# Attention softmax with the sink as a padded score column, a negated row maximum, and one transpose for each differential head

## The reference, cut to what matters

```python
# sliding window, per head: the sink takes part in the softmax, and its column is dropped
scores = q @ k.T * HEAD_DIM ** -0.5 - slope * dist          # -inf where masked
p = jax.nn.softmax(jnp.concatenate([scores, sink], axis=-1), axis=-1)[..., :-1]
out = p @ v

# differential, per head: two maps of scores, one product with v
s = q[m] @ k[m].T * HEAD_DIM ** -0.5 - slope * dist          # m = 0, 1; -inf where masked
p = jax.nn.softmax(s, axis=-1)
p_diff = p[:, :, 0] - lam * p[:, :, 1]
out = rms_norm(p_diff @ v, subln_g) * (1.0 - lambda_init)
```

## The time and the profile before

| what | value |
|---|---|
| median of 3 runs | 833.9 us |
| span of the profiled execution, first to last instruction | 831.0 us |
| so around the span, against the median of the runs | 2.9 us |
| PE busy | 780.1 us, 94% |
| DVE / ACT / POOL busy | 611.5 / 451.4 / 286.6 us |
| DMA, mean over the span | 162 GB/s |
| stretch of the attention steps | about 423 to 517 us from the span's start |
| mean granted TensorE clock | 0.985 |

### The profile page before, as it was taken

One profiled execution on the slowest core, in us unless ns is written; L12 is line 12 of the kernel. 1 busy time (PEld: TensorE's weight loads), 2 busy tenths in 40 slices (PEclk: granted clock), 3 DMA queues, 4 the chain that ended last, 5 costly groups with the idle time before them and its releaser, 6 DMA issues.

```text
span 831.0 us, 17788 instructions
## 1 busy us (share of the span) xinstructions
PE 780.1 (94%) x6332; PEld 764.7 (92%) x6332; DVE 611.5 (74%) x1077; ACT 451.4 (54%) x768; POOL 286.6 (34%) x174
## 2 busy tenths in 40 slices
PE   5989899799999999999899998699999999999994
PEld 5889899799999999999888877699999999999994
DVE  5899986867888887335867686589999999953332
ACT  7444454556555654436644555576666666644440
POOL 0366554463211221444665320742221222221231
PEclk9999999999999999999899999999999999999998
DMA  8444453455545566444342322525555555555531
GB/s 280 138 159 171 179 188 123 165 176 185 177 179 192 181 217 217 171 160 147 104 150 102 102 77 77 177 98 182 184 185 187 177 178 187 188 206 179 180 124 50
DMA packets 37631, 134.98 MB, mean 162 GB/s; under 512 B 4432, under 2 KB 4688, under 8 KB 37584
## 3 DMA queue, kind: packets, MB, share of 16 engines
q1 hardware_dynamic: 37584, 134.34, 46.8%
HBM read 133.28 MB, written 1.05 MB: 162 GB/s over the span
## 4 chain that ended last, share of the span: by engine, by line
PE 47%; DVE 8%; POOL 2%; ACT 2%; issue 2%; DVEq 0%; POOLq 0%; ACTq 0%
PE bank L1560 15%; PE bank L1561 15%; PE bank L1562 15%; POOL sumsq L507 1%; DVE tmp L1325 1%; DVE neg_max L1369 1%; ACT prob L883 1%; DVE row_max L1365 1%; POOL X L613 1%; DVE neg_max L1372 1%; DVE score L1360 1%; PE bank L1765 1%; PE bank L1773 1%; PE bank L1764 1%; DVE w_lo L967 1%
## 5 line engine op out<-in xcount | busy, mean ns | idle before, releaser
L1560 PE MATMUL bank<-h_hi,w_hi 128*128 128x256 f32 x1424 | 410.2, 288 | 23.2 <-DVE h_lo L979 13.5
L1561 PE MATMUL bank<-h_lo,w_hi 128*128 128x256 f32 x1424 | 406.1, 285 | 0.0
L1562 PE MATMUL bank<-h_hi,w_lo 128*128 128x256 f32 x1424 | 405.8, 285 | 0.0
L494 POOL TENSOR_TENSOR w_lo<-raw,w_hi 128x1024 fp32r<-128x1024 f32 (+2 forms) x86 | 211.6, 2463 | 434.0 <-ACT w_hi L643 433.9
L1560 PEld LDWEIGHTS bank<-h_hi,w_hi 128*128 128x128 f32 x1424 | 276.4, 194 | 30.2 <-DVE w_lo L967 12.0
L643 ACT ACTIVATE w_hi<-raw 128x1024 fp32r<-128x1024 f32 (+2 forms) x246 | 261.7, 1066 | 74.5 <-PE bank L1562 71.4
L967 DVE TENSOR_TENSOR w_lo<-raw,w_hi 128x1024 fp32r<-128x1024 f32 (+1 forms) x160 | 207.4, 1298 | 109.8 <-ACT w_hi L643 109.7
L1561 PEld LDWEIGHTS bank<-h_lo,w_hi 128*128 128x128 f32 x1424 | 276.7, 194 | 0.0
L1562 PEld LDWEIGHTS bank<-h_hi,w_lo 128*128 128x128 f32 x1424 | 276.5, 194 | 0.0
L1560 PE MATMUL bank<-f_hi,w_hi 128*128 128x256 f32 x432 | 121.5, 281 | 0.9 <-DVE f_lo L1234 0.9
L1561 PE MATMUL bank<-f_lo,w_hi 128*128 128x256 f32 x432 | 121.4, 281 | 0.0
(11 more groups left out here) (188 smaller groups left out, 771.7 us busy)
## 6 DMA issues: line engine op xcount, KB each, us to landing
raw<-in_w_up SPq DMA_DIRECT2D x108, 512.0 KB, 3.2
raw<-in_w_in SPq DMA_DIRECT2D x54, 512.0 KB, 3.3
raw<-in_w_down SPq DMA_DIRECT2D x32, 512.0 KB, 3.3
raw<-in_w_down SPq DMA_DIRECT2D x16, 704.0 KB, 4.1
raw<-in_w_o SPq DMA_DIRECT2D x8, 512.0 KB, 3.3
raw<-in_w_gate SPq DMA_DIRECT2D x8, 512.0 KB, 3.4
raw<-in_w_out SPq DMA_DIRECT2D x8, 512.0 KB, 3.3
raw<-in_w_b_out SPq DMA_DIRECT2D x4, 512.0 KB, 3.2
```

The costliest lines, as they stand in the source:

```text
L494: nc.gpsimd.tensor_tensor(w_lo[s][:, 0:n], raw[s][:, 0:n], w_hi[s][:, 0:n].bitcast(f32), ALU.subtract).then_inc(lo_ready[s], 1)
L1560: nc.tensor.matmul(ps, wh, hi[:, k, :], start=start and n == 0, stop=False)
L1561: nc.tensor.matmul(ps, wh, lo[:, k, :], start=False, stop=False)
L1562: last = nc.tensor.matmul(ps, wl, hi[:, k, :], start=False, stop=stop and n == len(ks) - 1)
```

## The change

- The score tile becomes `score[P, 8, 390]`: 8 slots, each of three pieces of 130 columns. In a sliding-window slot the columns behind the first and the second piece hold the sink (or -1e30), written once by POOL in `fill_pads`, during the stage `gate`. The row maximum and the exponentials with their sums run over the pieces and the pads, so the sink is in both. `sink_exp` and its addition go.
- The maximum is made with `negate=True` and written to `neg_max`. The third operation (L1369, L1372) goes.
- The exponentials are written in place. The wait of the bias for a free tile is now one on the transposes of the map 8 before.
- For a differential head DVE combines the two maps before the transpose: `first + mixing * second`, with `mixing = -lambda * sum(first) / sum(second)`. So one set of three transposes, one copy by ACT, one product with the values and one scaling stand for two. The group's transposes wait for the combination (`mixed`).
- The numbers of the semaphores follow: there are 12 groups g in place of 16 maps for the transposes, copies, products and outputs. They keep the steps of the last map of their group.
- `y_sq` shares the two tiles `cg`, so ACT waits for its own squares before the stage `up2`.

```diff
+GROUP_END = list(range(N_SWA)) + list(range(N_SWA + 1, N_MAPS, 2))
+PIECE = P + 2
     for m in range(N_MAPS):
-        steps[m + 3]["score"], steps[m + 4]["trans"], steps[m + 5]["pv"] = m, m, m
+        steps[m + 3]["score"], steps[m + 4]["sums"] = m, m
+    for g, m in enumerate(GROUP_END):
+        steps[m + 4]["trans"], steps[m + 5]["pv"] = g, g
...
+        def block_cols(m):
+            if m < N_SWA:
+                return ((0, P + 1), (PIECE, 3 * PIECE - 2))
+            return ((0, P), (P, 3 * P))
+        def pieces(m):
+            step = PIECE if m < N_SWA else P
+            return score[:, m % N_SWA, 0:3 * step].rearrange("p (n k) -> p n k", n=3)[:, :, 0:P]
...
+            def fill_pads():
+                pool.wait_ge(unit_done, UNIT0["gate"])
+                pool.wait_ge(const_in, 32)
+                nc.gpsimd.memset(score[:, :, 2 * PIECE - 2:2 * PIECE], -MASKED).then_inc(pads_done, 1)
+                pool.wait_ge(pads_done, 1)
+                for col in (P, 2 * PIECE - 2):
+                    nc.gpsimd.tensor_copy(
+                        score[:, 0:N_SWA, col].rearrange("p (j g) -> p j g", g=2),
+                        sinks[:].rearrange("p (g j) -> p j g", g=2)).then_inc(pads_done, 1)
...
             def exps(m):
-                act.wait_ge(negmax_done, m + 1)
-                if m >= 2:
-                    act.wait_ge(trans_done, m - 1)
+                act.wait_ge(negmax_done, 2 * (m + 1))
...
-                if kind == "swa":
-                    nc.scalar.activation(sink_exp[:, m, :], neg_max[:, m, :], ACT.Exp,
-                                         bias=sinks[:, h:h + 1]).then_inc(sink_done, 1)
...
+            act.wait_ge(y_ss_done, 10)
             up2 = ("conv_w_2", "conv_b_2")
...
                 dve.wait_ge(bias_done, m + 1)
-                for b, (lo, hi) in enumerate(((0, P), (P, 3 * P))):
-                    nc.vector.reduce_max(row_max[:, m, b:b + 1], score[m % 2][:, lo:hi], axis=AX.X
-                                         ).then_inc(max_done, 1)
-                dve.wait_ge(max_done, 2 * (m + 1))
-                if kind == "swa":
-                    nc.vector.tensor_scalar(neg_max[:, m, :], row_max[:, m, :], sinks[:, h:h + 1],
-                                            -1.0, ALU.max, ALU.mult).then_inc(negmax_done, 1)
...
+                for b, (lo, hi) in enumerate(block_cols(m)):
+                    nc.vector.tensor_reduce(neg_max[:, m, b:b + 1], score[:, m % N_SWA, lo:hi],
+                                            axis=AX.X, op=ALU.max, negate=True).then_inc(negmax_done, 1)
...
+                nc.vector.reciprocal(rden[:, m, :], row_sum[:, m, :]).then_inc(den_done, 1)
+                if part == 0:
+                    return
+                dve.wait_ge(den_done, DEN[m - 1] + 1)
+                dve.wait_ge(lam_step, 3)
+                nc.vector.scalar_tensor_tensor(mixing[:, h, :], rden[:, m, :], neg_lam[:, 0:1],
+                                               row_sum[:, m - 1, :], ALU.mult, ALU.mult
+                                               ).then_inc(den_done, 1)
+                dve.wait_ge(den_done, DEN[m])
+                first, second = score[:, (m - 1) % N_SWA, :], score[:, m % N_SWA, :]
+                for b, (lo, hi) in enumerate(block_cols(m)):
+                    nc.vector.scalar_tensor_tensor(first[:, lo:hi], second[:, lo:hi],
+                                                   mixing[:, h, b:b + 1], first[:, lo:hi],
+                                                   ALU.mult, ALU.add).then_inc(mixed, 1)
...
-            def transposes(m):
-                pe.wait_ge(exp_done, 2 * (m + 1))
+            def transposes(g):
+                m = GROUP_END[g]
+                if m < N_SWA:
+                    pe.wait_ge(exp_done, 2 * (m + 1))
+                    source = pieces(m)
+                else:
+                    source = pieces(m - 1)
+                    pe.wait_ge(mixed, 2 * (g - N_SWA + 1))
```

More of the change, by code:

```diff
@@ L296, in build @@
         ev = [sb(f"ev{i}", [P, TOK]) for i in range(4)]
-        cg = [sb(f"cg{i}", [P, TOK]) for i in range(2)]
+        cg_pair = sb("cg", [P, 2 * TOK])
+        cg, y_sq = [cg_pair[:, i * TOK:(i + 1) * TOK] for i in range(2)], cg_pair
         cv = [sb(f"cv{i}", [P, TOK]) for i in range(2)]
@@ L329, in build @@
         v_a, v_b = place("v_a", [P, 2, P]), place("v_b", [P, 2, 512])
-        score = [place(f"score{i}", [P, 3 * P]) for i in range(2)]
-        prob = [place(f"prob{i}", [P, 3 * P]) for i in range(2)]
+        score = place("score", [P, N_SWA, 3 * PIECE])
         prob_T = [place(f"prob_T{i}", [P, 3 * P]) for i in range(2)]
@@ L334, in build @@
         y_hi, y_lo = place("y_hi", [P, DC, TOK], f32r), place("y_lo", [P, DC, TOK], f32r)
-        y_sq = place("y_sq", [P, 512])
-        row_max = place("row_max", [P, 16, 2])
         neg_max = place("neg_max", [P, 16, 2])
         row_sum = place("row_sum", [P, 16, 2])
-        sink_exp = place("sink_exp", [P, 16, 2])
-        denom = place("denom", [P, 16, 2])
         rden = place("rden", [P, 16, 2])
+        mixing = place("mixing", [P, 4, 2])
         y_ss = place("y_ss", [P, 5, 2])
@@ L557, in _ @@
                     power("gate")
+                    fill_pads()
                 if c > 0:
@@ L1375, in denominators @@
             def denominators(m):
-                kind, _, part = MAPS[m]
-                n = DEN[m - 1] if m else 0
+                kind, h, part = MAPS[m]
                 dve.wait_ge(exp_done, 2 * (m + 1))
[L1379 to L1385, removed]
@@ L1386, in denominators @@
-                nc.vector.reciprocal(rden[:, m, :], total).then_inc(den_done, 1)
-                if kind == "diff" and part == 1:
-                    dve.wait_ge(den_done, n + 1)
-                    dve.wait_ge(lam_step, 3)
-                    nc.vector.tensor_scalar(rden[:, m, :], rden[:, m, :], neg_lam[:, 0:1], None,
-                                            ALU.mult).then_inc(den_done, 1)
-            def scaled_output(m):
-                kind, h, part = MAPS[m]
-                dve.wait_ge(pv_done, m + 1)
+                nc.vector.reciprocal(rden[:, m, :], row_sum[:, m, :]).then_inc(den_done, 1)
@@ new lines, in denominators, with scaled_output @@
+                for b, (lo, hi) in enumerate(block_cols(m)):
+                    nc.vector.scalar_tensor_tensor(first[:, lo:hi], second[:, lo:hi],
+                                                   mixing[:, h, b:b + 1], first[:, lo:hi],
+                                                   ALU.mult, ALU.add).then_inc(mixed, 1)
+            def scaled_output(g):
+                kind, h, part = MAPS[GROUP_END[g]]
+                m, width = GROUP_END[g] - part, HD if kind == "swa" else P
+                dve.wait_ge(pv_done, g + 1)
@@ L1396, in scaled_output @@
                 dve.wait_ge(den_done, DEN[m])
                 for b in range(2):
[L1398 to L1411 removed]
+                    y = (y_a if kind == "swa" else y_b)[:, b, width * h:width * (h + 1)]
@@ L1457, in _ @@
                         y_gained(c)
-                if step["trans"] is not None:
-                    denominators(step["trans"])
+                if step["sums"] is not None:
+                    denominators(step["sums"])
                 if step["pv"] is not None:
```

82 lines of the change are left out of this document (35 added, 47 removed).

## The result

| | before | changed |
|---|---|---|
| median of 20 runs each, taken side by side | 834.41 us (832.58 to 835.63) | 836.14 us (835.04 to 838.86) |
| profiled execution | span 831.0 us | 836.29 us, span 834.4 us |
| mean granted TensorE clock, profiled | 0.985 | 0.976 |

Ratio changed to before: 1.0027, interval 1.0019 to 1.0035. The changed kernel is slower by 1.6 to 2.9 us where the forecast was 0.5 us faster; its time is just above the range.

The account below looks back on a forecast made before the run. PE's own list, with short waits in it, was taken to bound the kernel. Span 831.0 - 2.2 (sliding -2.7, differential +0.5) + 1.7 for one clock fall = 830.5, with 2.9 to the median 833.4 us; range 831.2 to 836.0.

Parts of the forecast that it names:

- Base: Starting time of the kernel before: median taken as 833.9 us, with 2.9 us between profiled span and median.
- Sliding steps: Sliding-window attention steps: without the negation behind POOL, PE's waits for exponentials go, -2.7 us in all.
- Differential steps: Attention steps of differential heads: 4.4 us of PE work saved returns as waits for the combination, +0.5 us in sum.
- step 13: Differential attention, from the scores of map 9: chain through squares and combination to transposes, 6.7 us, before 5.60: +1.1.
- step 15: Differential attention: late bias, exponentials, squares, y_gained, then combination and transposes, 7.4 us, before 6.37: +1.0.
- step 17: Differential attention: chain through exponentials, y_hi, squares, combination and transposes, 6.4 us, before 5.59: +0.8.
- steps 19 and 20: Last attention steps up to the transpose of y: 8.1 us, before 6.20: +1.9.
- Steps 14 and 16: Differential attention steps without waiting transposes: 4.9 us, before 6.01 (-1.1), and 4.7 us, before 5.93 (-1.2).
- The combination: DVE's joining of two differential maps: 0.48 us for 256 columns, 0.35 for 128, bounds 0.42 to 0.63 us.
- third rival: Combinations on DVE slow, at half rate or behind POOL's power: 1.1 to 1.6 us more, about 834.8 us; chance 0.10.
- The clock: Behind PE's new waits in the differential attention steps: one fall to 1.2 GHz for 3.4 us, costing 1.7 us.
- second rival: Clock falls twice or more, or long, behind waits in differential attention: 835.1 to 836.8, say 836.0 us; chance 0.20.

## Why the prediction was wrong

**Base.** 833.9 us was the median of 3 runs, 834.41 us that of 20; and I took 2.9 us between span and median. In the changed kernel the profiled run of 836.29 us has a span of 834.4 us, 1.9 us less. So about 1 us of my 2.9 was that the profiled execution of before was a quick one. The error is small; it makes the time 0.5 us too low.

**Sliding steps, right.** 2.7 us expected, 2.73 measured. The signed maximum costs nothing that shows: 0.62 us for two passes, 0.61 without a sign. `fill_pads` is three operations of 0.11 to 0.17 us and POOL still stands idle 1.48 us behind them.

**Differential steps, right in mechanism, 0.5 us short.** Periods walked and measured: step 12 4.4 and 4.5, step 13 6.7 and 7.1, step 15 7.4 and 7.4, step 17 6.4 and 6.4, step 18 3.7 and 3.9, steps 19 and 20 8.1 and 7.8 us. Steps 14 and 16 were walked for full clock with 4.9 and 4.7 us; at full clock they are 5.0 and 4.8 us. The waits of 2.1, 2.5, 1.7 and 2.7 us read 2.4, 2.5, 1.8 and 2.0. The sum of +0.5 us is 54.75 - 3.0 - 50.68 = +1.1 us, most of it from step 13.

**The combination, right.** The source view has 350 to 479 ns, so 0.48 for 256 columns; a pair takes 0.74 us. The third rival did not come about. But I misread the case for it: 0.63 us is not the longest row of h_lo. The earlier trace rows is one of three groups in that view; another goes up to 964 ns. Four of its eight rows, beside POOL's `sumsq`, take 0.94 to 0.96 us, the other four 0.48 us:

```profile
394.51 1.96 POOL L507 TENSOR_TENSOR sumsq<-sq,sumsq 128x256 f32<-128x256 f32 x2 [0.70 <-ACT sq L660]
395.79 0.96 DVE L979 SCALAR_TENSOR_TENSOR h_lo<-X,gg,h_hi 128x256 fp32r<-128x256 f32 x1
```

So an operation of this kind can take twice its time beside POOL. That no combination did is luck: none ran beside w_lo or `sumsq`. The one at 509.96 ran inside POOL's power (509.68 to 510.37) and still took 0.74 us.

**The clock, wrong: "I count one."** This is the step that failed. The mechanism was right, the term was mis-sized: it measured two falls in each of four executions, two stretches twice and three twice, 3.0 or 4.5 us at 1.5 us each, where I put one of 1.7 us. That is the second rival, which I gave 0.20. The count rested on a comparison with two waits, one of 2.75 us that left the clock alone and one of 2.84 us that didn't, each read in one execution. This argument does not hold. With the same lists the wait of 2.75 us is followed by 0.50 in two of the four executions of the changed kernel. Falls stand behind waits of 2.41, 2.52, 2.06 and, with the scores first, 1.67 us, and the wait of 2.41 us is followed by one in two executions and by none in two others. So the length of one wait, read once, says little; the four waits together have nonetheless cost two falls each time.

**The sum.** Against 833.4 us, the clock adds 1.3 or 2.8 us, the differential steps 0.5 and the base 0.5: 2.3 to 3.8 us, where the median is 2.7 us above the forecast. The second rival's 836.0 us is next to the measured 836.14 us, partly by luck: its price of 1.7 us for a stretch is too high and its base and walk are too low.

**What I did not look for.** I priced the signed maximum for the sliding steps only. When the combination was taken away, the differential steps turned out 4.5 us shorter than before. The old trace has the stall there too: three of its eight negations take 1.85 to 1.87 us (471.98, 484.34 and 495.88), and PE waits 1.9 us for exponentials and 1.4 us for `y_scaled`; that all 4.5 us come from it isn't shown. The prediction compared the new steps with the old ones, so no term of its sum is missing. But it hid that the combination as placed loses 8.5 us by itself; seen apart, the two parts would have been a reason to drop or move the combination.

**Open.** What decides in an execution whether a given wait is followed by a fall isn't settled: the four profiles differ before 470 us too (falls at 97 us, at 148 us, or neither). How often the two patterns come in 20 runs can't be read from the times.

## What to carry to other kernels

Before an operation is put into a chain on which PE waits, read what stands ahead of it in the list of its engine: here one block moved to the front of DVE's step was worth 8 us, more than all matmuls saved. A wait that replaces matmuls costs its own length and then the clock behind it: 1.5 us for each stretch at half clock here. Take the falls from several profiles of one kernel, not from one; the same wait was followed by a fall in one execution and not in the next. When a sum meets the measurement to 0.2 us, check each term against the trace before you believe it, since here two errors cancelled. And time the parts of a change apart: this one was -7 and +9 us.

## What the runs showed of the hardware

- Granted clock: falls to 0.50 (1.2 GHz) behind PE waits of 1.67 to 2.5 us between lists with gaps of their own, not tied to the same wait from one execution to the next; 12 matmuls of 256 columns put into each of four waits kept it at 1.00 there. Each stretch of 3.4 us cost 1.5 us where PE had work throughout, and 0.5 us ahead of a wait for POOL, which shrank from 2.0 to 0.9 us.
- A small DVE operation with one SBUF input is held by POOL (0.17 us free, 1.85 us beside POOL's w_lo), the maximum over 128 or 256 columns of one SBUF input is not (0.61 us at 483.48 in the changed kernel, inside POOL's w_lo from 483.21 to 485.61). DVE's own w_lo takes 1.62 us where it meets POOL's work on X (435.98) and 1.22 us where it doesn't (465.37); no wait of PE shows for it.
- Two SBUF inputs with a scalar on DVE, with no w_lo or `sumsq` of POOL beside them, were not at half rate: 479 ns at most for 256 columns, 0.41 to 0.43 us for `copy_out` with one PSUM input. The Trainium skill, "Vector Engine (DVE) Microarchitecture Reference", section "Points that are easy to get wrong", has half the throughput for that; no run here shows it.
- In step 17 `mixing`, with SBUF inputs only, took 0.22 us inside POOL's power (499.62 to 500.31), as long as in step 15 outside it. The exclusive lock that the Trainium skill gives in "SBUF — State Buffer", section "SBUF: two separate sides", shows in the negation, in w_lo and in the h_lo of 0.96 us beside POOL's `sumsq` (0.48 us alone), not in this operation.
